# The embedding gate's opening products inside the expert branch in both layers, and the experts' last sums bank by bank

## What is computed

```python
x = x + mixer_block(rms_norm(x, ln_mix_g[i]), ...)
x = x + hier_moe(rms_norm(x, ln_ffn_g[i]), ...)        # 32 experts of 256 hidden columns, top 2 of a chosen group
h = rms_norm(x, ln_ple_g[i])
x = x + jax.nn.sigmoid(h @ w_ple_gate[i]) * (p[i] @ w_ple[i])   # the embedding gate
...
return rms_norm(x, final_norm_g)
```

## Time and profile before

| | us |
|---|---|
| median of 3 runs | 1143.59 |
| lowest and highest | 1140.56 and 1143.98 |
| span of the profiled execution (first to last instruction) | 1142.2 |
| TensorE busy in it | 1090.8 (95%) |
| VectorE, ScalarE, GpSimd busy | 649.1, 356.2, 134.8 |

### The profile page before, as it was taken

One profiled execution on the slowest core, in us unless ns is written; L12 is line 12 of the kernel. 1 busy time (PEld: TensorE's weight loads), 2 busy tenths in 40 slices (PEclk: granted clock), 3 DMA queues, 4 the chain that ended last, 5 costly groups with the idle time before them and its releaser, 6 DMA issues. The chain is left out here.

```text
span 1142.2 us, 21367 instructions
## 1 busy us (share of the span) xinstructions
PE 1090.8 (95%) x8168; PEld 859.8 (75%) x8168; DVE 649.1 (57%) x1353; ACT 356.2 (31%) x600; POOL 134.8 (12%) x163
## 2 busy tenths in 40 slices
PE   5999999999899999999989999999999999999996
PEld 5988998998765555554889799999887555555566
DVE  6687997455543333333777879975437333333356
ACT  4355442233331111111663454423334111111143
POOL 0121320011000001000002032101101000000000
PEclk9999999999999999999999999999999999999998
DMA  7558974546279999999454778663644999999962
GB/s 205 131 158 257 304 228 147 151 145 204 111 275 407 416 417 417 418 418 385 135 148 135 224 248 240 200 184 113 179 134 168 400 417 417 417 418 418 417 219 95
DMA packets 202981, 300.39 MB, mean 263 GB/s; under 512 B 14000, under 2 KB 166544, under 8 KB 186512
## 3 DMA queue, kind: packets, MB, share of 16 engines
q1 hardware_dynamic: 202896, 299.28, 73.9%
HBM read 298.21 MB, written 1.05 MB: 262 GB/s over the span
## 5 line engine op out<-in xcount | busy, mean ns | idle before, releaser
L738 PE MATMUL ps<-h_pair,wsplit 128*128 128x256 f32 x2880 | 370.6, 289 | 16.0 <-DVE h_pair L1845 7.4
L738 PEld LDWEIGHTS ps<-h_pair,wsplit 128*128 128x128 f32 x2880 | 356.9, 194 | 24.3 <-issue 15.1
L1836 DVE TENSOR_TENSOR wsplit<-ring,wsplit 128x1024 fp32r<-128x1024 f32 x136 | 167.4, 1235 | 64.6 <-ACT wsplit L1295 60.7
L1295 ACT ACTIVATE wsplit<-ring 128x1024 fp32r<-128x1024 f32 x136 | 141.5, 1055 | 198.6 <-PE ps L738 116.8
L738 PE MATMUL ps<-gu_ring,hT 128*64 128x256 f32 x896 | 107.6, 383 | 3.1 <-DMA gu_ring<-in_w_exp_up_dram 3.1
L1958 DVE SCALAR_TENSOR_TENSOR work<-work,convT 128x256 f32<-128x256 f32 x240 | 104.7, 508 | 0.0
L1522 ACT ACTIVATE prow<-ps 128x128 f32<-128x128 f32 x64 | 17.7, 277 | 277.9 <-PE ps L738 277.9
L738 PEld LDWEIGHTS ps<-gu_ring,hT 128*64 128x64 f32 x896 | 61.7, 137 | 47.7 <-issue 14.0
L2249 DVE TENSOR_TENSOR hT_r<-ps,hT_r 128x512 fp32r<-128x512 f32 x64 | 44.3, 692 | 88.2 <-ACT hT_r L1295 88.2
L2234 DVE TENSOR_TENSOR prow<-prow,ps 128x128 f32<-128x128 f32 x64 | 18.4, 288 | 131.7 <-ACT prow L1522 131.7
L738 PE MATMUL ps<-work,ring 128*128 128x256 f32 x384 | 85.7, 379 | 0.0
(11 more groups left out here) (213 smaller groups left out, 1149.6 us busy)
## 6 DMA issues: line engine op xcount, KB each, us to landing
ring<-in_w_in_dram SPq DMA_DIRECT2D x104, 512.0 KB, 4.6
down_ring<-in_w_exp_down_dram SPq DMA_DIRECT2D x40, 1024.0 KB, 19.1
gu_ring<-in_w_exp_gate_dram SPq DMA_DIRECT2D x28, 1024.0 KB, 14.8
gu_ring<-in_w_exp_up_dram SPq DMA_DIRECT2D x28, 1024.0 KB, 17.0
lent_down<-in_w_exp_down_dram SPq DMA_DIRECT2D x24, 1024.0 KB, 19.6
gu_last<-in_w_exp_gate_dram SPq DMA_DIRECT2D x12, 1024.0 KB, 14.0
gu_last<-in_w_exp_up_dram SPq DMA_DIRECT2D x12, 1024.0 KB, 16.2
ring<-in_w_exp_gate_dram SPq DMA_DIRECT2D x12, 1024.0 KB, 14.9
```

The source lines that it names most:

```text
L738: return nc.tensor.matmul(o, lhsT, rhs, start=first, stop=last)
L1295: return nc.scalar.activation(o, i, ACT.Copy)
L1836: TT(tile_split[:, m, 1, :, :], tile_of(name, m), tile_split[:, m, 0, :, :].bitcast(F32), ALU.subtract).then_inc(tile_low, 1)
```

## The change

Three edits. First, TensorE's `open_gate` of the first layer moves from behind the branch into both of its blocks, so that the jump over the second block comes after the 48 products of `pg0` and before `turn_vectors`. Second, the last `combine` goes bank by bank: the 8 products of banks 4 and 6, then the 8 of banks 5 and 7, with one signal of `bank_summed` for each bank instead of one of `summed` for all. Third, VectorE's sums, the rounding, and the products of `pg0` take the pairs in the order of the banks, 0, 2, 1, 3, and each sum waits for its own bank. SyncE and GpSimd wait for the fourth bank where they waited for `summed`.

```diff
+SUM_ORDER = (0, 2, 1, 3)
...
@@ combine (TensorE) @@
-                        for part in range(2):
-                            for i in range(4):
+                        def add(part, i, j):
+                            rows = slice(j * WIN, (j + 1) * WIN)
+                            return mm(two(ps[:, 4 + 2 * j + i // 2, :])[:, i % 2, :], outputs(k, per)[rows, part, i * P:(i + 1) * P],
+                                      window_sel[rows, k % 2, :], False, final and part == i % 2 == 1)
+                        if final:
+                            for half in range(2):
+                                for part, i in ((0, 2 * half), (0, 2 * half + 1), (1, 2 * half)):
+                                    for j in range(2):
+                                        add(part, i, j)
                                 for j in range(2):
-                                    rows = slice(j * WIN, (j + 1) * WIN)
-                                    last = mm(...)
-                        if final:
-                            last.then_inc(summed, 1)
+                                    last = add(1, 2 * half + 1, j)
+                                    last.then_inc(bank_summed, 1)
+                        else:
+                            for part in range(2):
+                                for i in range(4):
+                                    for j in range(2):
+                                        add(part, i, j)
@@ open_gate (TensorE) @@
-                        pair = (2 * i, 2 * i + 1)
+                        pair = (2 * SUM_ORDER[i], 2 * SUM_ORDER[i] + 1)
@@ the branch (TensorE) @@
                     keep_busy(3, 2)
                     if l + 1 == DEPTH:
                         gate_of_last()
+                    else:
+                        open_gate()
                 with pe.Else():
                     experts(WIDE)
                     if l + 1 == DEPTH:
                         gate_of_last()
+                    else:
+                        open_gate()
                 if l + 1 < DEPTH:
-                    open_gate()
                     rest_of_gate()
@@ add_sum (VectorE) @@
-                def add_sum(m):
+                def add_sum(i):
+                    m = SUM_ORDER[i]
+                    dve.wait_ge(bank_summed, 4 * l + i + 1)
                     x2 = xT[:, 2 * m:2 * m + 2, :]
                     TT(x2, two(ps[:, 4 + m, :]), x2, ALU.add).then_inc(x_added, 1)
@@ open_gate (VectorE) @@
                     low_tile(l, "pg0", 0)
-                    dve.wait_ge(summed, 1 * l + 1)
                     add_sum(0)
                     add_sum(1)
                     low_pair(0)
```

More of the change, by code:

```diff
@@ L458, in program @@
         tok_psum = lsem("tok_psum", DEPTH + 1)
-        summed = sem("summed")
+        bank_summed = sem("bank_summed")
         x_added = sem("x_added")
@@ L683, in _ @@
                     load_chunk(l, c)
-            sp.wait_ge(summed, 1 * (DEPTH - 1) + 1)
+            sp.wait_ge(bank_summed, 4 * DEPTH)
             sp.dma_start(gfull, final_norm_g.partition_broadcast(P)).then_inc(init_loaded, 16)
@@ L1176, in combine @@
                         pe.wait_ge(y_low, w + 1)
-                        for part in range(2):
-                            for i in range(4):
-                                for j in range(2):
-                                    rows = slice(j * WIN, (j + 1) * WIN)
-                                    last = mm(two(ps[:, 4 + 2 * j + i // 2, :])[:, i % 2, :], outputs(k, per)[rows, part, i * P:(i + 1) * P],
-                                              window_sel[rows, k % 2, :], False, final and part == i % 2 == 1)
-                        if final:
-                            last.then_inc(summed, 1)
+                        def add(part, i, j):
[7 more added lines that the diff above has]
+                                        add(part, i, j)
+                                for j in range(2):
+                                    last = add(1, 2 * half + 1, j)
[5 more added lines that the diff above has]
+                                        add(part, i, j)
                     def step(it, k, first, ending):
@@ L1546, in high_pair @@
                     act.wait_ge(x_added, 4 * l + i + 1)
-                    for c in (2 * i, 2 * i + 1):
+                    for c in (2 * SUM_ORDER[i], 2 * SUM_ORDER[i] + 1):
                         last = nc.scalar.activation(p_high[:, c, :], xT[:, c, :], ACT.Copy, scale=vcol("ple", c))
@@ L1731, in _ @@
                 if l + 1 < DEPTH:
-                    pool.wait_ge(summed, 1 * l + 1)
+                    pool.wait_ge(bank_summed, 4 * (l + 1))
                     pool.sem_clear(range(zeroed[0].num, zeroed[-1].num + 1))
```

## The result

| | before | with the change |
|---|---|---|
| median (lowest to highest), runs | 1142.28 us (1140.56 to 1147.68), 22 | 1145.24 us (1142.44 to 1146.93), 22 |
| ratio, 95% interval | | 1.0020 [1.0012, 1.0028] |
| the profiled execution | span 1142.2 us | time 1145.81 us, span 1144.0 us |

It says +2.3 us, from +1.4 to +3.2. The change costs time, less than the 0.3% that the prediction called "same", and its median lies inside the predicted range (1142.4 to 1149.2), 1.4 us under the forecast of 1146.6.

A forecast was written before the change was run, and what follows sets the result against it. TensorE was taken as the bound, busy 1090.8 of 1142.2 us. The jump's delay 2.85, the clock 1.5 and the banks 0 summed to +4.35 us, forecasting 1146.6 us, range 1142.4 to 1149.2.

The forecast's parts named there:

- The cases' frame: Whole kernel: chances of slower 0.41, same (within 0.3%, 3.4 us) 0.54, faster 0.05.
- the shorter jump: Rival: first layer's jump near 3.27 us, fetches missing the ring's load; +1.3 us, or +2.8 with the clock; chance 0.17.
- The own time: Base of the sum: the profiled execution at 1142.2 us, 1.4 us below the three runs' median, 1143.59.
- The sequencer is held by a wait: First layer's gate: the low tile's wait holds TensorE's sequencer; jump entered at 553.1, covered by 8 products, 1.0 us.
- The rival without a hold: First layer's gate: the low tile's wait does not hold the sequencer; jump entered near 551.5, +1.2 us, 1143.4; chance 0.13.
- The length of the jump: First layer's jump, TensorE: taken as 4.79 us, between row bounds of 3.27 and 4.79 us.
- The base: Transposes behind the first layer's gate: 555.15 before, 558.0 with the change, +2.85 us.
- The whole gain that can be had: First layer's gate: without a jump behind its products, the transposes would start at 553.97, 1.2 us before 555.15.
- The clock: TensorE behind the first layer's 4.0 us stop: granted clock falls, costing +1.5 us, bounded by 0 and 1.5.
- Paid 1 to 1: From the transposes to VectorE's copy of the spread: TensorE sets this handover, so the +2.85 us delay passes on in full.
- The sum: Whole kernel: 2.85 + 1.5 + 0 = +4.35 us on 1142.2, giving 1146.6; chance 0.42.
- The banks: Last sums, both layers: bank-by-bank signals gain 0, as VectorE's low tile hides about 0.6 us a layer.

The follow-up runs named there:

- the wait moved: The changed kernel with the last 8 products of `pg0`, which wait for the low tile, behind the first layer's jump; 1144.36 us, ratio 1.0011 to the kernel before.
- The near target: The changed kernel with TensorE's untaken block of the first layer emptied of its experts, so the jump is short; 1142.17 us, ratio 1.0000 to the kernel before.
- the two fills: The changed kernel with three more idle-keeping products between `open_gate` and the jump, run twice; 1144.49 and 1144.75 us, ratios 1.0023 and 1.0032 to the kernel before.
- the whole gate inside: All the first layer's gate ahead of the jump, on the changed kernel and the kernel before (old sums); 1141.18 and 1140.39 us, ratios 0.9983 and 0.9980.

## Why the prediction was right, and where

The cases' frame held (slower, but within 0.3%), and the mechanism is the predicted one. The sizes were less good than the number looks: +4.35 us were forecast and the ratio says +2.3 [1.4, 3.2]. What came is in size nearest to a rival, the shorter jump together with the clock's fall, +2.8 us. By its steps:

- **The own time.** The prediction set the profiled execution's time equal to its span, 1142.2 us. A run's time is 1.8 us above its span (1145.81 against 1144.0, 1139.06 against 1137.3), so that execution was near 1144.0 (the highest of the three runs is 1143.98), above the median and not below it. With that base the same sum gives 1148.4. That the span, 1142.2, is also what the median of more runs turned out to be (1142.28) is luck, and the forecast of 1146.6 owes its closeness in part to it.
- **The sequencer is held by a wait.** Right. The jump was taken to be entered 8.97 us after the sums (553.1); it was 8.8 with the change, at the first of the 8 products, and 7.7 with the wait moved. The rival without a hold had 7.4.
- **The length of the jump.** Mis-sized: 4.79 us taken, 3.33 to 3.88 in the three profiles of the change. The stop was 2.2 to 2.7 us and not 4.0, near the rival with a shorter jump.
- **The base.** Mis-sized by the same error: 11.02 us for the transposes came from the one profile with the long jump, and 9.9 is usual. So +2.85 us came out nearly right, by two errors that cancel: 12.24 to 12.79 less 9.89 is +2.4 to +2.9. Against the first profile alone it is 12.69 - 11.02 = +1.67.
- **"The whole gain that can be had", 1.2 us.** Wrong, and the step that the first profile misled most. The text itself had the reason in its hands: the low tile sets the last 8 products at 8.8, so a stop before the gate matters only beyond what they would wait for. With the jump's usual length it doesn't reach that far. The near target shows the true gain at the seam: its transposes stand where the kernel before has them in three of four profiles.
- **The clock.** Right in place and size: 1.5 us were forecast, and the 24 products took 1.5 us longer in four of the five profiles with an unfilled stop and 2.2 us in the other. Right for the seam, at least; the two fills kept the clock and their ratios did not fall. The profiles show a slow stretch at several other weak places, in some executions and not in others (with the change, the one behind the next layer's opening came in the first profile and not in the other two), and they blur a difference of this size. At the start of the next layer's spread the two profiles with the fill are still 1.4 us ahead of the change's three (48.9 against 50.3 us on the mean); from there to the last sums of the second layer all 14 profiles take 508.7 to 512.0 us, a spread of 3.2. Whether the 1.4 us are paid back there or are only lost in this spread stays open.
- **Paid 1 to 1.** Right at the next layer: its first product stands at 28.5 in the kernel before with the usual jump, and at 32.4 in the third profile of the change, +3.9, which is 2.35 of the jump and 1.55 of the clock. In the first pair of profiles VectorE's copy moved from 21.21 after the sums to 25.35, by 4.14 us, where the transposes had moved by 1.67: behind them come the 2.17 us of the slower 24 products and the rest of the slow stretch. Nothing on the way absorbed any of it. One detail is otherwise than forecast: the diagonal didn't move by the same amount but by 1.7 us (ready at 19.75, now at 21.44), since VectorE had stood still before it anyway, so its slack before the spread grew from 0.8 to 3.3 us.
- **The sum.** From the last sums of one layer to those of the next it is on the mean 557.2 us in the three profiles of the kernel before (557.3, 556.0, 558.2), and 560.5 in the three of the change (561.4, 560.6, 559.4): +3.3 us, 1 us under the forecast's +4.35. The ratio's +2.3 [1.4, 3.2] lies at that or somewhat below. At the next layer's spread it is 3.6 us on the same means (46.7 and 50.3). What is missing between that and 2.3 in the total is of the size of the spread named above.
- **The banks.** Right: VectorE's first sum follows the low tile with no idle time in the run with them alone, and neither there nor in the pair of kernels with the whole gate inside do the banks bring anything that the runs can tell.

## What to carry to other kernels

A long jump costs its length less the work that is queued when the sequencer enters it (here 3.3 to 3.9 us less 1.1), and a wait just ahead of it empties that queue: put it where the engine will wait for another engine anyway, here before the next layer's first rows, and the stop and the clock's fall after it lie under that wait. Before costing a jump from one profile, look for a second execution: its length differed by 1.4 us in the same place. And a stop that shows in the timeline is worth something only if the work behind it isn't held by something later, as the low tile held the gate here.

## What was not expected of the hardware

- The same jump, in the same place of the same kernel, took 3.40, 3.55 and 4.79 us, and over all runs with the far target 3.3 to 4.2 in the new places. In the 4.79 us case two instruction fetches fell in the stretch; in the first layer's far jump of all 12 other profiles it is one, and in the near one none. That the second fetch made that jump longer fits this, and was not tried. The Trainium skill, page Advanced Engine Details and Errata, section Control Flow Timing, gives some 51 ns for a branch that is always taken and some 108 ns for compare-and-branch; the near target took 307 ns here, and the measurement decides.
- The granted clock fell to 0.50 to 0.56, nearly all at its lower level, in a stretch behind every unfilled stop before the transposes (2.63, 2.74, 2.72 and 2.18 us) and behind the one of 3.14 us before the gate's last products (0.51), though the first profile had held it at 1.00 behind 2.07 us.
- Filling a stop so that the clock holds gave 1.5 us or more locally, and nothing that two sets of runs could find in the total.
